# A transformer layer on one core: first stages on TensorE column groups in another order, and the output projection as three fp32r products

## What is computed

```python
mod = jax.nn.silu(c) @ ada_w + ada_b                       # 1024 x 6144: shift, scale, gate, twice
h = rms_norm(x, norm1_g) * (1.0 + sc1) + sh1
proj = h @ w_in                                            # 1024 x 2888
ret = retention(rq, rk, rv)                                # 4 heads, then a norm and silu(rg) *
att = sparse_attention(aq, ak, av, iq, ik, iw)             # an index score per key, the 128 best kept
mix = jnp.concatenate([ret, att], axis=-1) * mix_scale
x = x + g1 * (mix @ w_o)                                   # 1024 x 1024: the output projection
h2 = rms_norm(x, norm2_g) * (1.0 + sc2) + sh2
y = moe(h2, router_w, router_b, w_gu, b_gu, w_down, b_down)  # 32 experts, 4 for each token
return rms_norm(x + g2 * y, final_g)
```

## Time and profile before

| | us |
|---|---|
| median of three runs | 1599.26 (1598.02 to 1599.36) |
| the profiled execution | 1597.53 |
| its span | 1595.7 |
| PE busy, of the span | 1483.2 (93%) |
| DVE busy | 1322.8 (83%) |
| ACT busy | 1090.0 (68%) |
| POOL busy | 422.4 (26%) |
| first matmul of the experts | at 398.49 |

### The profile page before, as it was taken

How to read it: one execution, slowest core, us unless ns; L and a number is a source line. 1 busy time by engine, 2 the same in 40 slices (tenths; PEclk the granted TensorE clock), 3 DMA queues, 4 the chain that set the end, 5 groups by cost and what they waited for, 6 DMA issues and landing times.

```text
span 1595.7 us, 20611 instructions
## 1 busy us (share of the span) xinstructions
PE 1483.2 (93%) x6872; PEld 1183.4 (74%) x6872; DVE 1322.8 (83%) x1137; ACT 1090.0 (68%) x1142; POOL 422.4 (26%) x341
## 2 busy tenths in 40 slices
PE   3999997895899999999999999999999999999983
PEld 2667964454688888888888888888888888888872
DVE  4689956266599999989999999999999999998992
ACT  3545237334677777888777777888877777788871
POOL 1113510102122222322233222332223323233221
PEclk8899998995899999999999999999999999999996
DMA  9745510325499999999999999999999999999974
GB/s 346 220 160 183 187 54 14 87 101 206 181 362 368 359 370 378 374 373 364 379 370 366 367 368 370 380 378 364 366 374 372 361 361 374 377 379 372 360 268 133
DMA packets 95983, 483.70 MB, mean 303 GB/s; under 512 B 23416, under 2 KB 32752, under 8 KB 43632
## 3 DMA queue, kind: packets, MB, share of 16 engines
q1 hardware_dynamic: 83200, 450.47, 72.7%
q0 software_dynamic: 12752, 32.84, 8.7%
HBM read 469.09 MB, written 23.61 MB: 309 GB/s over the span
## 4 chain that ended last, share of the span: by engine, by line
PE 83%; DVE 9%; ACT 3%; DMA 3%; issue 1%; SPq 0%; POOLq 0%; DVEq 0%; POOL 0%; ACTq 0%
PE bank L1366 15%; PE bank L1365 15%; PE bank L1367 15%; PE bank L1387 7%; PE bank L1389 7%; PE bank L1388 7%; PE bank L1248 3%; PE bank L1346 2%; PE bank L1358 2%; PE bank L1338 2%; DVE w_lo L1476 2%; DMA ring<-in_ada_w 1%; PE bank L1069 1%; PE bank L1070 1%; PE bank L1071 1%
## 5 line engine op out<-in xcount | busy, mean ns | idle before, releaser
L1515 DVE TENSOR_TENSOR e_lo<-ring,e_hi 128x2048 fp32r<-128x2048 f32 x384 | 868.6, 2290 | 94.5 <-ACT e_hi L742 94.1
L742 ACT ACTIVATE e_hi<-ring 128x2048 fp32r<-128x2048 f32 x384 | 728.4, 1914 | 236.7 <-PE bank L1367 235.4
L1365 PE MATMUL bank<-e_hi,x_hi 128*128 128x512 f32 x1024 | 406.0, 396 | 2.1 <-DVE e_lo L1515 2.1
L1366 PE MATMUL bank<-e_lo,x_hi 128*128 128x512 f32 x1024 | 402.6, 393 | 0.0
L1367 PE MATMUL bank<-e_hi,x_lo 128*128 128x512 f32 x1024 | 399.2, 390 | 0.0
L1365 PEld LDWEIGHTS bank<-e_hi,x_hi 128*128 128x128 f32 x1024 | 192.9, 188 | 48.9 <-DVE e_lo L1515 2.8
L1366 PEld LDWEIGHTS bank<-e_lo,x_hi 128*128 128x128 f32 x1024 | 193.1, 189 | 40.2
L1367 PEld LDWEIGHTS bank<-e_hi,x_lo 128*128 128x128 f32 x1024 | 192.9, 188 | 40.3
L1387 PE MATMUL bank<-e_hi,act_hi 128*128 128x512 f32 x512 | 208.4, 407 | 0.1
L1389 PE MATMUL bank<-e_hi,act_lo 128*128 128x512 f32 x512 | 202.0, 394 | 0.0
L1388 PE MATMUL bank<-e_lo,act_hi 128*128 128x512 f32 x512 | 201.2, 393 | 0.0
(11 more groups left out here) (246 smaller groups left out, 1786.4 us busy)
## 6 DMA issues: line engine op xcount, KB each, us to landing
ring<-in_w_gu SPq DMA_DIRECT2D x256, 1024.0 KB, 8.6
ring<-in_w_down SPq DMA_DIRECT2D x128, 1024.0 KB, 8.8
ring<-in_ada_w SPq DMA_DIRECT2D x24, 1024.0 KB, 7.3
ring<-in_w_in SPq DMA_DIRECT2D x9, 1024.0 KB, 5.9
ring<-in_w_o SPq DMA_DIRECT2D x4, 1024.0 KB, 7.1
ring<-in_w_in SPq DMA_DIRECT2D x10, 256.0 KB, 5.9
sum_rows<-xs POOLq DMA_DIRECT2D x5, 512.0 KB, 4.5
xs<-in_x SPq DMA_DIRECT2D x4, 512.0 KB, 5.0
```

What stands on the lines that cost most here:

```text
L742: return nc.scalar.activation(dst, src, ACT.Copy, scale=scale)
L1365: pe.matmul(bank[b][:], x_hi[:, c, :], hi, start=False, stop=False)
L1366: pe.matmul(bank[b][:], x_hi[:, c, :], lo, start=False, stop=False)
L1515: tt(e_lo[c % PARTS][:], raw(period.raw_slot(c)), e_hi[:, c % PARTS, :].bitcast(F32), ALU.subtract).then_inc(lo_ready, 1)
```

## The change

- *A and B on PE.* Each piece of `ada_w` becomes four matmuls with 32 output rows, 512 columns and silu(c) as weights, one on each group of 32 columns of the array (`mod_rows`). A goes to bank 0, B to bank 7, one bank for each half of B. The row is copied out, turned on PE and added. `modulate`, `rest_scale`, POOL's additions and L1059, L1145 and L1151 are gone.
- *Order of the first stages.* Four A pieces, the turned rows of x, the other four; `w_lo_part(0)` and `(1)` after the modulation; the steps of half 6 stand between the index scores, which have four banks of their own (3 to 6); the decay matrices and the sigmoids of the retention gates are made earlier.
- *Retention.* PE's heads overlap (`ret_scores` of the next head ahead of `ret_rows`).
- *w_o in two parts.* `wo_hi_part` on ACT and `wo_lo_part` on DVE, a quarter of w_o (128x2048) each: two quarters between the heads of retention, two in attention (`WO_AT`, steps 5 and 9). The mix is kept as `mix_hi` (ACT) and `mix_lo` (DVE, `mix_rest`).
- *Output projection.* `mixed` is 24 fp32r matmuls where it was 8 plain ones, and may start before the last two of the eight parts of the mix are there.
- *Router.* The rows that are turned are x itself and not the normalised ones; norm2's scale goes into the router's weights, the shift into its bias (a product of its own, `rb`), the root into `choose`. Turned rows are copied by two ACT instructions for each t where they were scaled by eight.
- *Smaller ones.* The bias parts of the experts are made in four pieces between the residuals; experts' first two chunks are loaded once w_o's slots are free, and not during retention.

The core of the diff:

```diff
+AFTER_MIX = ["o00", "rb"] + [f"o{t}{q}" for t in range(T - 1) for q in range(2)][1:] + ["l0", "o30", "c0", "l1", "o31"]
 AFTER_MIX += ["c1", "l2", "l3", "c2", "c3"]
+MIX_ORDER = [0, 1, 2, 3, 4, 6, 5, 7]
...
+WO_AT = [5, 9]
...
-                    elif c == 0:
-                        sp.wait_ge(g_stored, 16)
-                    elif 2 <= c < 5:
-                        sp.wait_ge(wo_used, c - 1)
+                    elif c < 5:
+                        sp.wait_ge(wo_used, (1, 2, 1, 2, 3)[c])
...
-            for i, n in enumerate(B_POOL):
-                k, half = n // 2, n % 2
-                o = acc[:, 2048 * half:2048 * half + 2048]
-                pool.wait_ge(rest_scaled, i + 1)
-                if k > 0:
-                    pool.wait_ge(rest_used[half], k)
-                nc.gpsimd.tensor_tensor(o, slot(LOAD_B[n]), o, ALU.add).then_inc(rest_used[half], 1)
...
+            def wo_hi_part(n):
+
+                r = LOAD_O[n]
+                a.wait_ge(landed[r % SLOTS], 16 * (r // SLOTS + 1))
+                if n == 0:
+                    a.wait_ge(w_lo_ready, W_HALVES)
+                    a.wait_ge(rest_used, 2 * KD)
+                if n == 2:
+                    a.wait_ge(dve_taken, D_RS + T * RH)
+                copy(wo_hi[n], slot(r)).then_inc(wo_hi_ready, 1)
 
             for h in range(RH):
+                if h in (1, 2):
+                    wo_hi_part(h - 1)
...
+                if h == 0:
+                    turned_rows(1)
...
+                if i in WO_AT:
+                    wo_hi_part(2 + WO_AT.index(i))
...
+            def mod_rows(b, n, k, used):
+
+                have(n)
+                for g in range(4):
+                    mm = pe.matmul(b[32 * g:32 * g + 32, :], sc_c[:, k:k + 1].broadcast_to((P, 32)),
+                                   slot(n)[:, 512 * g:512 * g + 512], start=(k == 0), stop=(k == KD - 1))
+                mm.then_inc(used, 1)
+                return mm
+
+            def rest_rows(low, high):
+
+                for i, n in enumerate(LOAD_B):
+                    if low < n < high:
+                        if i == KD:
+                            pe.wait_ge(mrow_ready, 2)
+                        mod_rows(bank[7], n, i % KD, rest_used)
...
+                    for kk in range(KD // 2, KD):
+                        mod_rows(bank[0], LOAD_A[kk], kk, ada_used)
+                    pe.wait_ge(mrow_ready, 1)
+                    for q in range(4):
+                        mm = pe.transpose(bank[0][:, q * P:(q + 1) * P], mrow[:, 0, q * P:(q + 1) * P], ident[:])
...
+                if n % 2 == 1 and n // 2 < KD:
+                    by_feature(A_AK, 6, P, [n // 2])
...
-            for m in range(16):
-                mm = pe.matmul(bank[7][:, m:m + 1], acc[:, 1024 + m * P:1024 + (m + 1) * P], ones[:, 0:1],
-                               start=True, stop=True)
-            mm.then_inc(mod_full, 1)
-            for n, at in enumerate((0, 512, 3072, 3584)):
-                j = D_GROW + n
-                dfree(j)
-                pe.matmul(dbank(j)[0:1, :], ones[:, 0:1], acc[:, at:at + 512], start=True,
-                          stop=True).then_inc(dve_full, 1)
...
+            ret_scores(0)
+            ret_scores(1)
+            ret_rows(0)
+            rest_turned(1)
+            ret_scores(2)
+            ret_rows(1)
+            ret_scores(3)
+            ret_rows(2)
+            ret_rows(3)
...
-                for k in range(KD):
-                    n = LOAD_O[k // 2]
-                    if (t, q) == (0, 0) and k % 2 == 0:
-                        have(n)
-                    w = slot(n).rearrange("p (k n) -> p k n", k=2)
-                    mm = pe.matmul(dbank(j)[:], hT[:, k, t * P:(t + 1) * P], w[:, k % 2, q * 512:(q + 1) * 512],
-                                   start=(k == 0), stop=(k == KD - 1))
-                    if (t, q) == (T - 1, 1) and k % 2 == 1 and k < KD - 1:
+                for n, k in enumerate(MIX_ORDER):
+                    if (t, q) == (0, 0):
+                        pe.wait_ge(mix_lo_ready, (6, 6, 6, 6, 6, 6, 8, 8)[n])
+                        pe.wait_ge(wo_lo_ready, k // 2 + 1)
+                    rows, cols = slice(t * P, (t + 1) * P), slice((k % 2) * D + q * 512, (k % 2) * D + q * 512 + 512)
+                    mm = exact(dbank(j)[:], mix_hi[:, k, rows], mix_lo[:, k, rows], wo_hi[k // 2][:, cols],
+                               wo_lo[k // 2][:, cols], n == 0, n == KD - 1)
...
+            def wo_lo_part(n):
+
+                v.wait_ge(wo_hi_ready, n + 1)
+                tt(wo_lo[n], slot(LOAD_O[n]), wo_hi[n].bitcast(F32), ALU.subtract).then_inc(wo_lo_ready, 1)
 
             v.wait_ge(decay_ready, RH)
             for h in range(RH):
+                if h >= 2:
+                    wo_lo_part(h - 2)
+                if h == 2:
+                    gate_rows()
...
+                if i - 1 in WO_AT:
+                    wo_lo_part(2 + WO_AT.index(i - 1))
+                if i == STEPS:
+                    mix_rest(2, 0, abank(A_MIX)[:])
+                if i - VALUE_LAG == 2 * T:
+                    mix_rest(0, 4, bank[6][:])
+                    mix_rest(1, 6, bank[7][:])
```

More of the change, by code:

```diff
@@ L436, in slot_free @@
                 elif which == "B":
[L437 to L438 removed]
+                    sp.wait_ge(rest_used, LOAD_B.index(n) + 1)
                 elif which == "W":
@@ L636, in _ @@
             pool.dma_start(sum_dram[S:S + P, :], xs[:, 0, :]).then_inc(sum_stored, 16)
+            pool.wait_ge(dve_full, D_["o31"] + 1)
+            done(nc.gpsimd.memset(xg, 0.0))
             pool.wait_ge(xn2_stored, 16 * T)
@@ L761, in _ @@
             copy(vecT[:], abank(j)[:, 0:72]).then_inc(act_taken, 1)
-            def rest_scale(low, high):
-                for n in B_POOL:
-                    k, r = n // 2, LOAD_B[n]
-                    if low < r < high:
-                        a.wait_ge(landed[r % SLOTS], 16 * (r // SLOTS + 1))
-                        copy(slot(r), slot(r), sc_c[:, k:k + 1]).then_inc(rest_scaled, 1)
             def w_hi_part(h):
@@ L835, in _, with rows_out_of_bank, turned_rows @@
                 w_hi_part(16 + m)
+            def rows_out_of_bank(half):
+                a.wait_ge(rest_used, KD * (half + 1))
+                copy(mrow[:, half, :], bank[7][:]).then_inc(mrow_ready, 1)
+            def turned_rows(half):
+                j = (A_M0, A_M1)[half]
+                src = abank(j).rearrange("p (j g r) -> p g j r", j=4, r=32)[:, 2 - 2 * half:4 - 2 * half, :, 0]
+                take(j, modB[:, 8 * half:8 * half + 8].rearrange("p (g j) -> p g j", g=2), 1.0, src)
+            rows_out_of_bank(0)
             for m in range(2):
@@ L899, in values_out @@
                     k = 4 + 2 * n + half
-                    copy(hT[:, k, :], bank[6 + n][:], vecT[:, 64 + k:65 + k]).then_inc(values_taken, 1)
+                    copy(mix_hi[:, k, :], bank[6 + n][:], vecT[:, 64 + k:65 + k]).then_inc(mix_hi_ready, 1)
             def retention_out(k):
@@ L1251, in mixed, with router_bias @@
                         mm.then_inc(wo_used, 1)
                 mm.then_inc(dve_full, 1)
+            def router_bias():
+                pe.wait_ge(router_in, 32)
+                pe.wait_ge(affine_ready, 2)
+                j = D_["rb"]
+                dfree(j)
+                for k in range(KD):
+                    mm = pe.matmul(dbank(j)[:, 0:E], modB[:, k:k + 1].broadcast_to((P, P)), rw[:, k, :],
+                                   start=(k == 0), stop=(k == KD - 1))
+                mm.then_inc(dve_full, 1)
@@ L1450, in _ @@
             v.wait_ge(csig_ready, 1)
-            done(tt(sc_c[:], cs[:], csig[:], ALU.mult))
+            tt(sc_c[:], cs[:], csig[:], ALU.mult).then_inc(silu_ready, 1)
             v.wait_ge(rms_root, 1)
             nc.vector.reciprocal(ri[:, 0:T], rt[:, 0:T]).then_inc(rms_inv, 1)
-            def modulate(n, at, k, used):
-                v.wait_ge(landed[n % SLOTS], 16 * (n // SLOTS + 1))
-                o = acc[:, at:at + 2048]
-                if k == 0:
-                    ins = ts(o, slot(n), sc_c[:, k:k + 1], None, ALU.mult)
-                else:
-                    ins = stt(out=o, in0=slot(n), scalar=sc_c[:, k:k + 1], in1=o, op0=ALU.mult, op1=ALU.add)
-                ins.then_inc(used, 1)
-            def rest_sum(low, high):
-                for k in range(KD):
-                    if low < LOAD_B[2 * k] < high and 2 * k not in B_POOL:
-                        modulate(LOAD_B[2 * k], 0, k, rest_used[0])
-                        v.wait_ge(rest_used[0], k + 1)
             def w_lo_part(h):
-                if h % 2 == 0 and h > 0:
-                    rest_sum(LOAD_W[h // 2 - 1], LOAD_W[h // 2])
                 v.wait_ge(w_hi_ready, h + 1)
@@ L1477, in w_lo_part @@
                    ALU.subtract).then_inc(w_lo_ready, 1)
[L1479 to L1483 removed]
+            v.wait_ge(ada_used, KD)
+            nc.vector.tensor_copy(mrow[:, 0, :], bank[0][:]).then_inc(mrow_ready, 1)
```

(9 more changed lines are left out.)

288 lines of the change are left out of this document (166 added, 122 removed).

## The result

| | before | after |
|---|---|---|
| median, us (lowest to highest, 12 runs each) | 1597.26 (1595.16 to 1599.70) | 1601.76 (1598.60 to 1603.44) |
| the profiled execution, us | 1597.53 | 1602.62 |
| its span, us | 1595.7 | 1600.6 |
| first matmul of the experts, at us | 398.49 | 403.17 |

The account below looks back on a forecast made before the run. Only the first 398 us change, with the bound shifting by stage (loads, then engine round trips, PE alone in the output projection). Terms -14.1 + 12 + 7 - 12 = -7 gave 1592 us; own range 1587 to 1597, 80% range 1580 to 1605.

Parts of the forecast that it names:

- first stage, to the first index score: Start of the kernel: with modulation rows made on PE, h starts at 34.4 us, not 40.76; -6 us.
- scores and half 6: Index scores: PE does scores, half 6 and three B pieces in one stretch of 19.5 us for 22.2; -2.7 us.
- projections: Projections: 13 B pieces added, later small matmuls, low-half waits and 3.4 us of slower clock removed; -5.4 us.
- retention: Retention: w_o quarters make DVE wait for ACT and PE for DVE, +9.3, and slower clock, +3; +12 us.
- attention, and 1.4 us up to the projection's start: Attention: DVE's quarters +4.6, mix_rest about +2, last turn +0.5, so +7; output projection starts 1.4 us earlier.
- output projection, to the first expert: Output projection: cheaper products, norm off the router's path, -10.5 us with slower clock; -12 including the earlier start.
- The last A piece is there at 30.8: First stage: the last A piece of ada_w is loaded by 30.8 us, as before the change.
- rival B: Pieces of ada_w: column groups run two at a time, 20 pieces 0.87 us longer each; 1609 us, chance 0.12.
- rival D: Projections: no gain, as DVE waits for high halves, ends late and retention waits; 1597 us, chance 0.10.
- rival A: Retention and attention: w_o quarters cost nothing, retention -2, attention +2; 1573 us, half of it, 1583, likelier; chance 0.18.
- the norm is off the path to the router, which is worth a few us at the last block: Output projection: the router no longer waits for the norm, saving a few us at the last block.
- C: Retention and attention: quarters cost more through loop delays and falling clock, +17 and +12; 1602 us, chance 0.15.

Follow-up runs that it names:

- Experiment 6: Changed kernel with GpSimd's four loads of ada_b bias rows issued behind the decay masks, not at the start: 1599.81 us, ratio 1.0014 to the kernel before.
- experiment 5: Changed kernel with the transposed vectors in bank 7, so PE's first ada_w pieces don't wait for ACT's copy: 1601.56 us, ratio 1.0028 to the kernel before.
- experiment 2: Changed kernel with six unused fp32 matmuls ahead of the last retention score of heads 2 and 3: 1598.21 us, ratio 1.0003 to the kernel before.
- experiment 1: Changed kernel with DVE's low quarter of w_o behind the decay of heads 2 and 3 in retention: 1586.26 us, ratio 0.9926 to the kernel before.
- experiment 3: Changed kernel with attention's two low quarters of w_o on DVE moved to steps 8 and 12: 1596.87 us, ratio 0.9996 to the kernel before.
- Experiment 7: Changed kernel with block 3's logits ahead of block 1's places and GpSimd's zeroing moved to DVE's last norm wait: 1598.36 us, ratio 1.0005 to the kernel before.

## Why the prediction was wrong

| term of the sum | forecast, us | measured in the two traces | off by |
|---|---|---|---|
| first stage, to the first index score | -6 | 76.95 - 81.01 = -4.1 | 1.9 |
| scores and half 6 | -2.7 | 20.2 - 21.5 = -1.3 | 1.4 |
| projections | -5.4 | -9.6 in all up to retention, so -4.2 | 1.2 |
| retention | +12 | 38.4 - 24.1 = +14.3 | 2.3 |
| attention, and 1.4 us up to the projection's start | +7 - 1.4 | 60.57 - 52.22 = +8.4 | 2.8 |
| output projection, to the first expert | -10.6 | 95.50 - 103.91 = -8.4 | 2.2 |
| sum | -7 | +4.7 | 11.7 |

The third column is from one execution of each kernel. No term had the wrong sign and none was off by more than 3 us; all six were off to the same side. The order of waits in retention was as described, down to PE's two of 5 to 6 us; three steps were wrong in kind and not only in size: the loads of the first stage, attention without a term for the clock, and the gain from the norm at the end. A sum of six large terms with both signs came out at -7, and the forecast's own range, 1587 to 1597, took no account of their errors lying to one side (1601.76 is inside the wider one, 1580 to 1605). In the main I gave each gain its full size and each loss its bare one:

- *First stage.* The step that failed is "The last A piece is there at 30.8". I listed what PE, DVE and ACT do and kept the loads of before, and didn't count the four loads that the change puts at the start, though they stand in the diff. The piece was there at 34.16. Experiment 6 shows the four loads to be worth 2.8 of these 3.4 us, and experiment 5 that the slots are worth 0.7 at most. That h then starts at 34.42, where I had 34.4, is in part luck: the piece is still 0.6 us late (31.36), and what follows it takes 3.1 us and not the 3.6 that I added up.
- *Scores.* I set 19.5 us, counted from the first score, against 22.2 that begin 0.8 us ahead of it, at 80.20; from the first score (81.01) to the end of half 6 the kernel before takes 21.5. The other 0.7 is the stretch itself, 20.2 and not 19.5.
- *Projections.* A piece in a row of pieces takes 0.90 us (three from 77.58, the next matmul at 80.29) as I took it; alone between other matmuls it takes 1.0 (102.81 to 103.81), and 13 of them were busy for 13.2 us, not 11.7. The four groups do run at once, so rival B (two at a time, 1.73) is out. The rule of the Trainium skill (TensorE: Matmul & The Clock Gate, Part 3: Packing small matmuls), from which I had estimated 1.1, isn't borne out for a row of pieces: there the weight loads (the next four at 78.03) run beside the matmuls, with column groups of full height. For a piece by itself it comes nearer. The slow clock that I took out as 3.4 us is 4.0 by my own numbers (110.9 - 54.4 - 46 - 6.5), so that the term should have been -6.0. DVE ended its rounds at 202 and PE never waited for a low half, so rival D is out.
- *Retention.* Order: forecast +9.3 with PE's gain taken off; experiment 2, with the clock restored, has 33.5 - 24.1 = +9.4. The clock: I allowed 3 us, it was 4.9. That the loss as a whole is DVE's place for the low quarter is shown by experiment 1: without it this stage is 2.2 us shorter than before, the "-2" of rival A.
- *Attention.* DVE's quarters lie almost in full on the loop (PE's two waits of 3.23 were 1.03 and 1.35, so 4.1 for the 4.6 counted), and around `mix_rest` two more waits grow by 2.5 together (2.57 and 1.56, which were 1.08 and 0.59), as counted. The step that failed is the clock, to which I gave no term: the first values take 4.54 instead of 2.38, so 2.2 us, and experiment 3, without the wait, has them at 2.38. In the trace of before the second values already took 4.07, behind a wait of 1.35 us, where the earlier trace rows has others at 2.37.
- *Output projection.* The step "the norm is off the path to the router, which is worth a few us at the last block" failed: the logits of block 3 stand behind the `places` of block 1 on PE, which wait for DVE, so that nothing came of it; and GpSimd's zeroing, moved there by the change, stops a cast of DVE for 1.26 us. Experiment 7 gives both back, 3.6 us. The products were mis-sized too: 5.45 us each forecast, 5.6 to 5.7 measured (316.85, 322.52, 328.12), with the granted clock at 1.00; over eight that is 1.6 us. Why one fp32r matmul takes 0.234 us here and 0.227 in the projections isn't shown.

The nearest rival was C (1602: the quarters cost more, since each delay goes round the loop once more and the clock falls), with a chance of 0.15. That its total is right is luck, since it has less than half of the cause: retention and attention cost 5 us more than counted, not the 10 of their upper bounds, and 6.7 us came from gains that were smaller.

The same change, with the instructions of a few places in another order, is 29 us faster than the kernel before (1569.38 for 1598.21 on the same chip). Its gains of 9.6 us up to retention and 8.4 in the output projection were real; the losses were a matter of where a few groups of instructions and loads stand.

## What to carry to other kernels

When work is added to an engine that has idle time, ask at which instruction it waits, and put the work exactly there: the same 2.3 us on DVE cost 8 us a piece ahead of the decay and left no wait behind it. Price a gap on PE with the slower matmuls behind it (here 4.9 us behind 10.8 us of waiting, and 2.2 behind 3.2), but as a range: the second wait of 3.2 in attention cost no more clock than the 1.35 before it had, and the values behind the one of 2.57 took 2.37 us, as at full clock. And go through the queue of each engine that the diff moves a DMA or a fill on, since those are easily taken for free. Where a forecast is the small difference of large terms, let the range hold the case in which all of them err to one side.

## What the runs showed of the hardware

- With 128 packets of 2 KB from GpSimd's queue (0.26 MB) beside it, the other queue moved 3.76 MB in 12 us (3.90 in experiment 5) where it moved 4.81 without them (4.78 in the kernel before): their cost is not their bytes.
- Twice six fp32 matmuls of no use, put into waits of 5.9 and 4.9 us, made a kernel 3.5 us faster: the granted clock stayed at 1.00 (2.4 GHz) where it was 0.70 in the mean and 0.53 in the rows of head 1, which is the lower level, 1.2 GHz, for most of them.
- With GpSimd's memset of 128x1024 beside it a cast of four columns on DVE took 1.43 us, and ended with the memset (371.20 and 371.17); with the memset elsewhere, beside GpSimd's DMA issues alone (experiment 7), it took 0.17 us. The Trainium skill (SBUF — State Buffer, Who interferes with whom) describes a port pair that a GpSimd instruction holds until it ends; the common end agrees with it. That the profile has the cast begin 0.43 us ahead of the memset isn't explained by it.
- Four fp32 matmuls of 32 output rows on four column groups, each with its own weight load, take 0.90 us a set where three sets stand in a row (77.58 to 80.29); one plain fp32 matmul of 512 columns takes 0.866.
